# Merge gates computed inside the prompt's attention, a reordered projection, and an expert ring of sixteen slots

## The chip, the cores and the metric

The kernel runs on one core of one Trainium2 chip. The metric is the device time of one execution in microseconds (us). The time before is the median of three runs.

## The reference, cut to what matters

One layer handles a prompt of 256 tokens and eight sample tokens (T = 264 tokens together), with a model width of 1024. One input projection yields the columns of an RWKV branch (a), of a sparse-attention branch (b) and of the merge gates (g); the branches are mixed under the gates, and a mixture of 32 experts follows.

```python
def merge_and_ffn(x, y_a, y_b, p_g, w_br_a, w_br_b, w_out, norm_ffn, w_router, b_router, w_up, b_up, w_down, b_down):
    g_a, g_b = jnp.split(jax.nn.sigmoid(p_g), 2, axis=-1)
    x = x + (g_a * (y_a @ w_br_a) + g_b * (y_b @ w_br_b)) @ w_out
    return x + moe_ffn(rms_norm(x, norm_ffn), w_router, b_router, w_up, b_up, w_down, b_down)
...
        p_a, p_b, p_g = split_cols(rms_norm(xp, norm_attn[layer]) @ w_in[layer], MIX_COLS)
        y_a, wkv_p, shift_p = rwkv_branch(p_a, ...)
        y_b, cmp_p, sel_p, win_p = nsa_prompt(p_b, cw, rel_bias)
        xp = merge_and_ffn(xp, y_a, y_b, p_g, *mw)
```

`moe_ffn` sends each token to four of 32 experts; an expert is `clamped_swiglu(x @ w_up[e] + b_up[e]) @ w_down[e] + b_down[e]` with `w_up[e]` 1024x2048 (8 MB in f32) and `w_down[e]` 1024x1024 (4 MB). `nsa_prompt` attends with compressed, selected and window keys; the new window cache of the samples (`win_s`) is the old one moved by one token.

## The kernel before, in words

Everything is f32. The program is a row of stages, and each stage is a block in which every engine has its own instruction queue written out by hand; all engines meet at the end of a block. The stages in order: projection, RWKV in chunks of 64 tokens ("chunks"), compression of the cache pages, `attend_prompt`, `attend_samples`, merge, `route`, the experts, and a final norm.

**Projection** (`project`). The projected activations lie transposed in `pT[:, j, :]`, one tile j of 128 columns by 264 tokens; there are 41 tiles, 0 to 13 for branch a, 14 to 23 for branch b, 24 (GT, 24 columns) for its gates, and 25 to 40 (MT and up) for the merge gates. SP (SyncE) loads the weights two tiles at a time into `w_group`, three buffers of 1 MB. TensorE (PE) computes a tile as eight matmuls over the contraction (L460); each f32 matmul shows as two records in the trace, so a tile is 16 records. ScalarE (ACT) evicts each tile into `pT` (`evicted(a, b)`), the merge gates with a sigmoid. Between the tiles PE turns small pieces into token rows: `kv` turns (L492), `shift` turns (L498), sample rows (L507) and the token products (L520) for the chunks. Their copies out of PSUM are on VectorE (DVE); the last are fed by a long chain of elementwise work on DVE (from L399 to L412, signal `tin`), which begins when ACT has taken the square roots of `sqk`. The input of the projection is `hT`, the normed input turned, and it lives only in this stage. GpSimd (POOL) ends the stage by writing the shift states and by queueing the 4 MB copy of the window cache from DRAM to DRAM (`win_copied`).

**attend_prompt**. The 16 units are (head, half of the prompt). For the unit i, PE computes scores (L1241), DVE adds bias and takes the row maximum, ACT takes the exponentials (L1148), DVE scales, PE turns the probabilities (`turn`, L1099), ACT and DVE copy them out of PSUM to `probsT` (L1154), PE multiplies by the values (`values`, L1266 and L1268). PE's queue runs `scores(i+1)`, `turn(i)`, `values(i)`. Ahead of the units stand the compressed scores (L1221) and the turns of their probabilities `cmp_p` (L1099), whose copies to `cmp_pT` are on DVE (L1180). In the stage POOL issues 16 indirect gathers of selected cache blocks for the samples.

**attend_samples** holds `win_rows`, the window keys of eight samples (4 MB). **merge** multiplies the branch outputs, left in PSUM, with the gates on DVE, adds, and multiplies with `w_out`.

**Experts**. `B["ring"]` has twelve slots of 1 MB: eight for `w_up[e]`, four for `w_down[e]`. SP loads in the order up(1), down(0), then up(e), down(e-1); each load of a slot waits until PE has used the slot (`up_used`, `down_used`). The eight slots of up(0) are loaded in `route`. PE's queue is up(e), `turn_x(e+1)`, down(e-1) (L1964, L1945, L1982); ACT, DVE and POOL do the activation between up and down, gather the token rows and scatter the results.

## Time and profile before

| | |
|---|---|
| median of 3 runs | 1788.57 us (1782.23 to 1802.88) |
| profiled execution, own time | 1795.35 us |
| its span | 1793.5 us |
| mean granted TensorE clock, share of full | 0.901 |
| instructions | 21221 |
| busy: PE matmul, PE weight load | 1382.3 us (77%), 696.5 us (39%) |
| busy: DVE, ACT, POOL | 372.5 us (21%), 224.1 us (12%), 169.9 us (9%) |
| read from HBM, written | 484.37 MB, 16.95 MB |

The profiled execution is one of its own beside the three timed runs and is 6.8 us above their median. Stages read from the timeline: projection 0 to 213.4 us, chunks to 325.6, compression to 440.5, attend_prompt to 562.8, attend_samples to 612, merge to 693, route to 755.5, experts to 1743.2, final norm to 1793.5. In the rows, PEclk is the share of its full speed that the TensorE clock was granted, PEld is the weight load, and "idle n <- X y" names what ended n us of idle time ahead of an instruction.

### The profile page before, as it was taken

The page shows a single profiled execution, that of the slowest core. Times are in us where ns is not written, and L with a number is a line of the kernel's source. Part 1 is how long each engine was busy: PE and PEld are TensorE (multiplying, and loading weights), DVE is VectorE, ACT ScalarE, POOL GpSimd, SP SyncE. Part 2 cuts the span into 40 slices and gives each one's busy share as a digit, 9 for nine tenths or more (in the row PEclk, how much of TensorE's full clock was granted, in tenths as well). Part 3 has the DMA queues.
Part 4 walks back from the last instruction along what each step waited for, and adds up shares of the span by engine and source line. Part 5 has one row for each costly group of instructions (what it writes and reads, how often), then busy time and mean ns, then how long its engine had stood idle before and what let it go on. Part 6 is the DMA issues. An engine that isn't in the chain of part 4 may idle for free. (4 is left out here: it accounts for less than half of the span.)

```text
span 1793.5 us, 21221 instructions
## 1 busy us (share of the span) xinstructions
PE 1382.3 (77%) x8102; PEld 696.5 (39%) x8103; DVE 372.5 (21%) x792; ACT 224.1 (12%) x479; POOL 169.9 (9%) x226
## 2 busy tenths in 40 slices
PE   6978976499689595497878887887877887877870
PEld 5867876266577484332222222222222222222220
DVE  3341174311333322510101010010101010010104
ACT  2221111022122103210000000000000000000001
POOL 1000061211200000000010100000010100000010
PEclk9989988698556897599999999999999999999995
DMA  5326231531402225299999999999999999999973
GB/s 171 118 87 218 74 76 29 122 107 49 178 1 94 113 100 170 92 370 416 417 418 416 419 415 419 416 418 416 418 416 417 418 415 418 414 418 414 418 282 133
DMA packets 128400, 489.60 MB, mean 273 GB/s; under 512 B 18750, under 2 KB 50752, under 8 KB 94896
## 3 DMA queue, kind: packets, MB, share of 16 engines
q1 hardware_dynamic: 117304, 457.15, 64.8%
q0 software_dynamic: 10640, 31.11, 4.9%
q8 instruction: 41, 0.67, 0.1%
q10 hardware_dynamic: 400, 0.55, 0.1%
q14 instruction: 15, 0.12, 0.0%
HBM read 484.37 MB, written 16.95 MB: 280 GB/s over the span
## 5 line engine op out<-in xcount | busy, mean ns | idle before, releaser
L1964 PE MATMUL bank<-ex_ring,ex_xT 128*64 128x512 f32 x2048 | 495.6, 607 | 138.1 <-DMA ex_ring<-in_w_up 136.5
L1964 PEld LDWEIGHTS bank<-ex_ring,ex_xT 128*64 128x64 f32 x2048 | 126.4, 136 | 478.5 <-DMA ex_ring<-in_w_up 319.3
L1982 PE MATMUL bank<-ex_ring,ex_hT 128*64 128x512 f32 x1024 | 247.1, 604 | 47.3 <-DMA ex_ring<-in_w_down 46.6
L1921 DVE TENSOR_SCALAR ex_g<-bank 128x512 f32<-128x512 f32 x32 | 22.1, 691 | 656.8 <-PE bank L1970 656.8
L460 PE MATMUL bank<-hT,w_group 128*128 128x264 f32 (+1 forms) x656 | 153.9, 397 | 6.0 <-DMA w_group<-in_w_in 5.4
L1982 PEld LDWEIGHTS bank<-ex_ring,ex_hT 128*64 128x64 f32 x1024 | 62.4, 136 | 209.2 <-DMA ex_ring<-in_w_down 128.2
L460 PEld LDWEIGHTS bank<-hT,w_group 128*128 128x128 f32 (+1 forms) x656 | 126.3, 194 | 31.0 <-DMA w_group<-in_w_in 5.8
L1866 POOL DMA_INDIRECT scratch_choice<-ex_y,ex_di x32 | 33.3, 1040 | 675.1 <-ACT ex_y L1896 675.1
L1882 ACT ACTIVATE ex_xT<-bank 128x512 f32<-128x512 f32 x33 | 19.7, 597 | 337.7 <-PE bank L1945 337.7
L1886 ACT ACTIVATE ex_hT<-bank 128x512 f32<-128x512 f32 x32 | 19.1, 597 | 311.2 <-PE bank L1951 301.1
L1896 ACT ACTIVATE ex_y<-bank 128x512 f32<-128x512 f32 x32 | 19.1, 597 | 266.4 <-PE bank L1987 266.4
L1932 DVE COPY ex_pick_down<-ex_pick 96x64 bf16 x31 | 5.9, 191 | 223.0 <-PE bank L1987 223.0
L1858 POOL DMA_INDIRECT ex_xg<-scratch_h,ex_si x33 | 34.5, 1045 | 41.1 <-POOL ex_si L1853 24.3
L306 ACT ACTIVATE pT<-bank 128x264 f32<-128x264 f32 (+1 forms) x41 | 15.6, 389 | 150.2 <-PE bank L460 150.2
L1241 PE MATMUL bank<-pT 64*128 64x128 f32 (+1 forms) x64 | 26.0, 562 | 9.8 <-DVE cmp_pT L1180 9.8
L1266 PE MATMUL bank<-kvtok,probsT 128*128 128x64 f32 x96 | 24.7, 430 | 9.3 <-ACT probsT L1154 9.3
L1009 DVE COPY pT<-bank 128x256 f32<-128x256 f32 x32 | 13.6, 425 | 87.0 <-PE bank L1080 86.7
L1573 PE MATMUL bank<-mixed,w_out_sb 128*128 128x264 f32 x128 | 28.7, 387 | 1.5 <-DVE mixed L1547 1.5
L1080 PE MATMUL bank<-masks,x 128*128 128x128 f32 x96 | 18.7, 328 | 14.4 <-PEq L120 14.4
L1080 PE MATMUL bank<-masks,blocks 128*128 128x128 f32 x160 | 29.5, 309 | 0.0
L1565 PE MATMUL bank<-yaT,w_branches 128*128 128x264 f32 x64 | 17.5, 421 | 14.4 <-DMA w_branches<-in_w_br_b 14.4
L1945 PE MATMUL bank<-masks,ex_xg 128*128 128x128 f32 x132 | 22.1, 291 | 7.6 <-DMA ex_xg<-scratch_h,ex_si 7.6
(456 smaller groups left out, 1362.0 us busy)
## 6 DMA issues: line engine op xcount, KB each, us to landing
ex_ring<-in_w_up SPq DMA_DIRECT2D x256, 1024.0 KB, 17.2
ex_ring<-in_w_down SPq DMA_DIRECT2D x256, 512.0 KB, 18.2
w_group<-in_w_in SPq DMA_DIRECT2D x20, 1024.0 KB, 5.1
win_rows<-in_state_win_kv SPq DMA_DIRECT2D x8, 512.0 KB, 7.3
w_out_sb<-in_w_out SPq DMA_DIRECT2D x1, 4096.0 KB
choice_rows<-scratch_choice SPq DMA_DIRECT2D x2, 2048.0 KB
out_win_s<-in_state_win_kv POOLq DMA_DIRECT2D x1, 4088.0 KB, 24.2
x<-in_x_prompt SPq DMA_DIRECT2D x4, 512.0 KB
```

The source lines that it names most:

```text
L460: mm = mmul(banks[2 + i % 4][0:n, 0:T], w[:, g % 3, kc, c:c + n], hT[:, kc, :], start=(kc == 0), stop=(kc == KD - 1))
L1080: mm = mmul(banks[u % 3][:, P * t:P * t + P], raw[p % 3][:, t, c0:c0 + P], ident, start=True, stop=True)
L1241: mm = mmul(banks[i % 2][:, TP * br:TP * br + P * (tt + 1)], qg[gs, r, P * tt:P * tt + P], pT[gs, KVT + 2 + 2 * br, 0:P * (tt + 1)], start ...
L1266: mmul(b[:, HD * br:HD * br + HD], pTs[:, i % 2, c:c + P], kvtok[:, kt, 384 + 256 * br + HD * g:384 + 256 * br + HD * g + HD], start=(kt = ...
L1573: mm = mmul(banks[m % 2][:, 0:T], wo[:, c, P * m:P * m + P], mix[:, c, :], start=(c == 0), stop=(c == KD - 1))
L1858: pool.indirect_dma_start(B["xg"][:], None, halves(scratch["h"]), bass.IndirectOffsetOnAxis(ap=B["si"][:, 0:1], axis=0), bounds_check=last ...
L1866: pool.indirect_dma_start(halves(scratch["choice"]), bass.IndirectOffsetOnAxis(ap=B["di"][:, 0:1], axis=0), B["y"][:], None, bounds_check= ...
L1882: nc.scalar.activation(B["xT"][:].rearrange("p a b -> p (a b)"), banks[6][:], ACT.Copy).then_inc(S["xT_ready"], 1)
L1921: nc.vector.tensor_scalar(g[:], banks[0][:], 7.0, None, ALU.min).then_inc(S["g_ready"], 1)
L1945: mm = nc.tensor.transpose(banks[6][:, P * k:P * k + P], B["xg"][:, P * k:P * k + P], ident)
L1964: mm = mmul(banks[n // 2][lo:lo + SLOTS, :], B["xT"][:, k % 4, SLOTS * (k // 4):SLOTS * (k // 4) + SLOTS], B["ring"][:, k, 512 * n:512 * n ...
L1982: mm = mmul(banks[4][SLOTS * n:SLOTS * n + SLOTS, :], B["hT"][:, k % 4, SLOTS * (k // 4):SLOTS * (k // 4) + SLOTS], B["ring"][:, 8 + j, D ...
```

## The change

- The 16 merge-gate tiles leave the projection. `hT` is kept up to the attention. In `attend_prompt` SP loads the gate weights, 1 MB for two tiles, into the two halves of `w_cmp` (the compression's first weight), and PE computes gate tiles 0 to 2 after the compressed scores, tile 3 after the turns of `cmp_p`, and tiles 4 to 15 one in each of the units 0 to 11, between `turn(i)` and `values(i)`. ACT evicts them with tanh(x/2), and the merge makes the sigmoid of it: DVE adds 1 in the same instruction that multiplies, and the half goes into the next eviction's scale.
- In the projection ACT takes the square roots after 14 tiles instead of 18; PE turns the shift states after tile 19 and ahead of the kv turns, which come after the last tile.
- The 4 MB window copy moves from the end of the projection to the start of the chunk stage, ahead of POOL's first work there.
- `Dg` of the chunks and one buffer of the compression lie in the free gate tiles of `pT`; two of the eight samples' windows lie in `hT`, and their loads follow in the same order.
- The ring has 16 slots: eight for up, two times four for down. `route` loads down(0) as well as up(0), down(1) is issued as the experts start, and SP's order is then up(e), down(e). The expert loop on PE and SP runs in pairs. The small buffers share one array, which is also the room for the routed rows `h`, and `hit` shares `h_T`.

```diff
+            C["hT"] = sb(front, "hT", [P, KD, T])
...
-                hT = sb(st, "hT", [P, KD, T])
+                hT = C["hT"]
...
-                groups = [[12, 13], *([j, j + 1] for j in (4, 6, 0, 2, 8, 10, 18, 20, 22, 14, 16)), [GT], *([j, j + 1] for j in range(MT, NT, 2))]
...
                 group_of = {j: g for g, ts in enumerate(groups) for j in ts}
...
-                    pool.dma_start(o["win_s"][0, :, 0:511].rearrange("b t a g d -> b (t a g d)"),
-                                   a["state_win_kv"][0, :, 1:512].rearrange("b t a g d -> b (t a g d)")).then_inc(win_copied, 16)
...
-                    evicted(10, 18)
+                    evicted(10, 14)
...
+                    evicted(14, 17)
...
-                    evicted(18, 33)
+                    evicted(17, 25)
                     for i, dst in enumerate((vt, av[:, :, 0, :], br[:, :, 0, :], ktt)):
-                        evicted(33 + 2 * i, 35 + 2 * i)
...
-                    projected(14, 22)
-                    pe.wait_ge(evict, 20)
+                    projected(14, 20)
                     pe.wait_ge(kks, 4)
+                    for i in range(4):
+                        for j in range(min(4, NA_T - 4 * i)):
+                            mm = nc.tensor.transpose(banks[aux[i]][0:9, P * j:P * j + P], pT[:, 4 * i + j, TP - 1:T], ident)
+                        mm.then_inc(shp, 1)
+                    projected(20, 25)
                     for i in range(6):
                         t0, n = TILES[i // 2]
-                        if i >= 4:
+                        if i < 4:
+                            pe.wait_ge(sh_ok, i + 1)
+                        else:
                             pe.wait_ge(kv_ok, i - 3)
                         for j in range(3):
                             mm = nc.tensor.transpose(banks[aux[i % 4]][0:n, P * j:P * j + P], pT[:, KVT + 3 * (i % 2) + j, t0:t0 + n], ident)
                         mm.then_inc(kvp, 1)
-                    projected(22, 25)
-                    pe.wait_ge(kv_ok, 6)
-                    for i in range(4):
-                        for j in range(min(4, NA_T - 4 * i)):
-                            mm = nc.tensor.transpose(banks[aux[i]][0:9, P * j:P * j + P], pT[:, 4 * i + j, TP - 1:T], ident)
-                        mm.then_inc(shp, 1)
```

```diff
-                    projected(25, 29)
-                    pe.wait_ge(sh_ok, 4)
                     pe.wait_ge(smr.sem, 1)
                     for i, src in enumerate((wsm[:], kk[:, :, TP:T], cum[:, :, TP:T], q["k2"][:, :, TP:T], v[:, :, TP:T], r[:, :, TP:T])):
...
-                    pe.wait_ge(sm_ok, 6)
...
-                        projected(33 + 2 * i, 35 + 2 * i)
...
+                            else:
+                                pe.wait_ge(sm_ok, (5, 6, 3, 4)[2 * i + tt])
...
+                    pool.dma_start(o["win_s"][0, :, 0:511].rearrange("b t a g d -> b (t a g d)"),
+                                   a["state_win_kv"][0, :, 1:512].rearrange("b t a g d -> b (t a g d)")).then_inc(win_copied, 16)
                     pool.wait_ge(C["idx_ok"], 8)
                     cmp_piece(pool, 0)
...
+                w = C["w1"][:].rearrange("p a b c -> p (a b c)").rearrange("p (r k n) -> p r k n", r=2, k=KD)
...
+                NG, AHEAD = NT - MT, 4
+                gate_bank = lambda t: banks[4 + t % 2] if t < AHEAD else banks[6 + t % 2]
...
+                    for g in range(NG // 2):
+                        if g >= 2:
+                            sp.wait_ge(mtd, 2 * (g - 1))
+                        c0 = 3096 + 256 * g
+                        sp.dma_start(w[:, g % 2], a["w_in"][0][:, c0:c0 + 256].rearrange("(k p) n -> p k n", p=P)).then_inc(w_in[g % 2], 16)
...
+                    def gate(t):
+                        act.wait_ge(mtd, t + 1)
+                        nc.scalar.activation(pT[:, MT + t, :], gate_bank(t)[:, 0:T], ACT.Tanh, scale=0.5).then_inc(mte, 1)
+
+                    gate(0)
                     act.wait_ge(cx, 1)
                     nc.scalar.activation(pc[:].rearrange("p a b c d -> p (a b c d)"), pc[:].rearrange("p a b c d -> p (a b c d)"), ACT.Exp).then_inc(cxe, 1)
+                    for t in range(1, AHEAD):
+                        gate(t)
...
+                        if 1 <= i <= NG - AHEAD:
+                            gate(AHEAD + i - 1)
...
+                    def gate(t, lo, hi):
+                        if lo == 0:
+                            pe.wait_ge(w_in[t // 2 % 2], 16 * (t // 4 + 1))
+                            if t >= 2 and t != AHEAD and t != AHEAD + 1:
+                                pe.wait_ge(mte, t - 1)
+                        for kc in range(lo, hi):
+                            mm = mmul(gate_bank(t)[:, 0:T], w[:, t // 2 % 2, kc, P * (t % 2):P * (t % 2) + P], C["hT"][:, kc, :], start=(kc == 0), stop=(kc == KD - 1))
+                        if hi == KD:
+                            mm.then_inc(mtd, 1)
+
+                    for t in range(AHEAD - 1):
+                        gate(t, 0, KD)
                     pe.wait_ge(cp, 1)
                     for j in range(4):
                         if j >= 2:
...
+                    gate(AHEAD - 1, 0, KD)
...
                             pe.wait_ge(oe, i - 1)
+                        else:
+                            pe.wait_ge(mte, AHEAD - 1 + i)
...
                         turn(i)
+                        if i < NG - AHEAD:
+                            gate(AHEAD + i, 0, KD)
                         values(i)
...
+                        step(stt(ta[:, m % 2, :], pT[:, MT + m, :], 1.0, banks[2 * (m % 2)][:, 0:T], ALU.add, ALU.mult))
```

```diff
+            work = sb(moe, "ex_work", [P, 8, 512])
+            for name, shape, dt in (("ring", [P, 16, 2 * FF], F32), ("bias", [96, 3 * FF], BF16), ("pick", [96, NEXP + 1], BF16),
...
+            S["ring_in"] = [sem(f"ring_in{i}") for i in range(16)]
...
                     for k in range(8):
                         sp.dma_start(B["ring"][:, k, :], a["w_up"][0][0, P * k:P * k + P, :]).then_inc(S["ring_in"][k], 16)
+                    for k in range(8):
+                        sp.dma_start(B["ring"][:, 8 + k // 2, D * (k % 2):D * (k % 2) + D], a["w_down"][0][0, P * k:P * k + P, :]).then_inc(S["ring_in"][8 + k // 2], 16)
...
-                    def down(e, wait):
+                    def down(e, half, wait):
                         for j in range(4):
+                            slot = 8 + 4 * half + j
                             if wait:
-                                sp.wait_ge(S["down_used"], 4 * (e - 1) + j + 1)
+                                sp.wait_ge(S["down_used"], 4 * (e - 2) + j + 1)
                             for c in range(2):
                                 r0 = 256 * j + P * c
-                                sp.dma_start(B["ring"][:, 8 + j, D * c:D * c + D],
+                                sp.dma_start(B["ring"][:, slot, D * c:D * c + D],
                                              a["w_down"][0][bass.ds(e, 1), r0:r0 + P, :].rearrange("e p n -> (e p) n")
-                                             ).then_inc(ring_in[8 + j], 16)
-
+                                             ).then_inc(ring_in[slot], 16)
+
+                    down(1, 1, False)
                     up(1, True)
-                    down(0, False)
-                    with sp.Fori(2, NEXP) as e:
-                        up(e, True)
-                        down(e - 1, True)
-                    down(NEXP - 1, True)
+                    with sp.Fori(1, NEXP // 2) as pair:
+                        for half in range(2):
+                            up(2 * pair + half, True)
+                            down(2 * pair + half, half, True)
 
```

How the instructions stand in each engine's queue shows in what follows; each line is the program's line, the operation, its output and input, and its count. A matmul of the order is two records in the trace.

TensorE in the projection before, from tile 14 on. `w_group` marks projection tiles (eight matmuls a tile), L492 the kv turns, L498 the shift turns, L507 the sample rows, L520 the token products:

```order
L460 MATMUL bank<-hT,w_group 128x264 x64
L492 MATMUL bank<-masks,pT 128x128 x12
L492 MATMUL bank<-masks,pT 8x128 x6
L460 MATMUL bank<-hT,w_group 128x264 x16
L460 MATMUL bank<-hT,w_group 24x264 x8
L498 MATMUL bank<-masks,pT 9x128 x14
L460 MATMUL bank<-hT,w_group 128x264 x32
L507 MATMUL bank<-masks,sample_decay 8x128 x4
L507 MATMUL bank<-masks,w_cmp 8x128 x8
L507 MATMUL bank<-masks,rw_k 8x128 x4
L507 MATMUL bank<-masks,shifted 8x128 x8
L460 MATMUL bank<-hT,w_group 128x264 x48
```
and after, the same stretch (L459 tiles, L487 shift turns, L497 kv turns):

```order
L482 MATMUL bank<-rw_at_rt,masks 128x264 x4
L459 MATMUL bank<-hT,w_group 128x264 x48
L487 MATMUL bank<-masks,pT 9x128 x14
L459 MATMUL bank<-hT,w_group 128x264 x32
L459 MATMUL bank<-hT,w_group 24x264 x8
L497 MATMUL bank<-masks,pT 128x128 x12
L497 MATMUL bank<-masks,pT 8x128 x6
L508 MATMUL bank<-masks,sample_decay 8x128 x4
L508 MATMUL bank<-masks,w_cmp 8x128 x8
L508 MATMUL bank<-masks,rw_k 8x128 x4
L508 MATMUL bank<-masks,shifted 8x128 x8
L520 MATMUL bank<-masks,shifted 64x64 x32
```
The groups of 48, 32 and 16 gate matmuls that stood between the rows and between the products are gone, and the shift turns stand ahead of tile 20.

TensorE at the start of the prompt's attention before (L1221 compressed scores, L1099 turns, L1241 scores, L1266 and L1268 values):

```order
L1221 MATMUL bank<-KcT,pT 128x8 x16
L1099 MATMUL bank<-masks,cmp_p 8x128 x16
L1241 MATMUL bank<-pT 128x128 x2
L1241 MATMUL bank<-pT 128x256 x2
L1099 MATMUL bank<-masks,scores 128x128 x2
L1266 MATMUL bank<-kvtok,probsT 128x64 x2
L1268 MATMUL bank<-Vc,cmp_pT 128x64
L1241 MATMUL bank<-pT 128x128 x2
```
and after (L1242, L1101, L1276, L1303 and L1305 in the same roles; L1251 is a gate tile, with its weights in `w_cmp`):

```order
L1242 MATMUL bank<-KcT,pT 128x8 x16
L1251 MATMUL bank<-hT,w_cmp 128x264 x24
L1101 MATMUL bank<-masks,cmp_p 8x128 x16
L1251 MATMUL bank<-hT,w_cmp 128x264 x8
L1276 MATMUL bank<-pT 128x128 x2
L1276 MATMUL bank<-pT 128x256 x2
L1101 MATMUL bank<-masks,scores 128x128 x2
L1251 MATMUL bank<-hT,w_cmp 128x264 x8
L1303 MATMUL bank<-kvtok,probsT 128x64 x2
L1305 MATMUL bank<-Vc,cmp_pT 128x64
```
Three tiles stand ahead of the turns of `cmp_p`, one behind them, and one in every unit between its turns and its values.

ScalarE in the same stage after (L1155 is the gate's eviction by tanh, L1159 and L1167 are exponentials, L1175 is the copy to `probsT`):

```order
L1155 ACTIVATE pT<-bank 128x264
L1159 ACT_TABLE_LOAD
L1159 ACTIVATE cmp_p<-cmp_p 128x128
L1155 ACTIVATE pT<-bank 128x264 x3
L1167 ACTIVATE scores,row_sum<-scores,row_max 128x128 x2
L1175 ACTIVATE probsT<-bank 128x256
L1167 ACTIVATE scores,row_sum<-scores,row_max 128x256 x2
L1155 ACTIVATE pT<-bank 128x264
L1175 ACTIVATE probsT<-bank 128x512
```
The gate's evictions stand one behind each unit's exponentials, ahead of the copy; there is one table load in the stage, as before.

SyncE around the start of the experts before, and then after:

```order
L1646 DMA ex_ring<-in_w_up 128x2048 x8
L1649 DMA scratch_h<-h_rows 128x1024 x2
L1649 DMA scratch_h<-h_rows 8x1024
L1604 UNCONDITIONAL_BRANCH
L1818 UNCONDITIONAL_BRANCH
L1824 DMA ex_ring<-in_w_up 128x2048 x8
L1833 DMA ex_ring<-in_w_down 128x1024 x8
```
```order
L1691 DMA ex_ring<-in_w_up 128x2048 x8
L1693 DMA ex_ring<-in_w_down 128x1024 x8
L1696 DMA scratch_h<-ex_work 128x1024 x2
L1696 DMA scratch_h<-ex_work 8x1024
L1649 UNCONDITIONAL_BRANCH
L1865 UNCONDITIONAL_BRANCH
L1881 DMA ex_ring<-in_w_down 128x1024 x8
L1871 DMA ex_ring<-in_w_up 128x2048 x8
```
The eight loads of down(0) now stand in `route` ahead of the rows' store, and the first loads of the experts' block are those of a down weight instead of an up weight.

## Rows read from the trace of the kernel before

**Rows 1.** Windows: length; busy (x) of PE, PEld, DVE, ACT, POOL; PEclk; DMA share; GB/s.
```profile
110.60:213.40 102.80, 87.56 (x616) 71.31 (x616) 20.28 (x28) 12.89 (x30) 1.67 (x3) 0.92 0.40 133
...
467.50:562.80 95.30, 84.77 (x288) 67.87 (x288) 35.19 (x112) 22.48 (x80) 0.00 (x0) 0.50 0.02 9
```

**Rows 2.** Timeline of the projection: start, us, engine, line.
```profile
81.93 18.41 PE L460 MATMUL bank<-hT,w_group 128*128 128x264 f32 x82
...
99.41 0.71 DVE L399 TENSOR_SCALAR rw_at_rt<-rw_at_rt 128x1056 f32<-128x1056 f32 x1 [17.49 <-ACT rw_at_rt L334]
119.20 1.22 DVE L412 TENSOR_TENSOR rw_a<-rw_bt_kt,chunk_decay 128x1024 f32<-128x1024 f32 x1
121.08 1.44 PE L492 MATMUL bank<-masks,pT 128*8 128x128 f32 x6 [7.63 <-DVE kvtok L416]
...
151.30 3.67 DVE L423 COPY pT<-bank 8x512 f32<-8x512 f32 x6 [13.57 <-PE bank L507]
165.94 16.54 PE L460 MATMUL bank<-hT,w_group 128*128 128x264 f32 x64 [5.37 <-DMA w_group<-in_w_in]
...
182.41 2.08 PE L520 MATMUL bank<-masks,shifted 64*64 64x64 f32 x64
```

**Rows 3.** Window of 10 us inside the projection.
```profile
60.00:70.00 10.00, 10.00 (x47) 8.54 (x46) 5.85 (x13) 2.67 (x7) 0.00 (x0) 1.00 0.50 166
```

**Rows 4.** Timeline of the chunk stage.
```profile
219.31 1.13 DVE L672 TENSOR_SCALAR block_rows<-pages,cols 128x2 uint32<-128x2 int32 x8 [5.78 <-DMA cols<-in_c_cols]
255.45 3.93 POOL L650 TENSOR_TENSOR rw_bt_kt<-sample_sa,sample_vec 128x2048 f32<-128x2048 f32 x1 [14.33 <-DVE sample_sa L711]
```

**Rows 5.** The weight loads L252 from 120 to 170 us.
```profile
DMA to landing us min/median/max: 4.9/11.4/18.0
```

**Rows 6.** Timeline at the start of the prompt's attention.
```profile
440.52 6.13 PE L1221 MATMUL bank<-KcT,pT 64*128 64x8 f32 x32 [1.01 <-PEq L913]
451.40 6.29 PE L1099 MATMUL bank<-masks,cmp_p 128*8 128x128 f32 x32 [4.75 <-DVE cmp_p L1177]
466.77 0.68 DVE L1180 COPY cmp_pT<-bank 8x512 f32<-8x512 f32 x1 [7.06 <-DMA out_shift_s<-bt_tok_rb]
467.51 2.93 PE L1241 MATMUL bank<-pT 64*128 64x128 f32 x8 [9.83 <-DVE cmp_pT L1180]
```

**Rows 7.** Windows after the turns L1099 of cmp_p, while TensorE is idle.
```profile
458.00:460.00 2.00, 0.00 (x0) 0.00 (x0) 0.68 (x1) 0.00 (x0) 1.39 (x3) 1.00 1.02 418
460.00:462.00 2.00, 0.00 (x0) 0.00 (x0) 0.00 (x0) 0.00 (x0) 1.70 (x2) 0.56 1.04 418
```

**Rows 8.** Windows: one pair of units; a dense stretch of turns.
```profile
480.45:492.23 11.78, 10.62 (x38) 8.50 (x37) 4.39 (x14) 2.81 (x10) 0.00 (x0) 0.50 0.00 0
570.00:580.00 10.00, 10.00 (x89) 9.04 (x89) 4.29 (x10) 3.11 (x7) 0.00 (x0) 1.00 0.55 224
```

**Rows 9.** Waits inside the sixteen units: total, times, longest.
```profile
PE bank L1266 <- ACT probsT L1154: 9.3, 16, 0.7
```

**Rows 10.** Windows from the end of routing to the last load.
```profile
728.00:755.50 27.50, 9.17 (x42) 8.29 (x42) 19.28 (x50) 2.76 (x1) 0.00 (x0) 0.50 0.00 1
755.50:766.50 11.00, 5.69 (x16) 2.19 (x18) 0.70 (x2) 0.60 (x1) 3.25 (x6) 0.50 0.07 20
766.50:1720.00 953.50, 772.96 (x3422) 219.67 (x3418) 91.56 (x185) 72.37 (x124) 75.27 (x122) 1.00 1.02 416
1720.00:1741.20 21.20, 17.05 (x80) 5.15 (x80) 2.96 (x6) 2.22 (x4) 1.23 (x2) 1.00 0.75 278
```

**Rows 11.** Timeline of the experts' end on TensorE.
```profile
1720.36 1.94 PE L1964 MATMUL bank<-ex_ring,ex_xT 128*64 128x512 f32 x8 [0.39 <-DMA ex_ring<-in_w_up]
1723.25 1.94 PE L1982 MATMUL bank<-ex_ring,ex_hT 128*64 128x512 f32 x8
1733.89 3.65 PE L1982 MATMUL bank<-ex_ring,ex_hT 128*64 128x512 f32 x16 [0.69 <-ACT ex_hT L1886]
1741.18 1.94 PE L1982 MATMUL bank<-ex_ring,ex_hT 128*64 128x512 f32 x8 [1.18 <-DMA ex_ring<-in_w_down]
```

79 lines of the change are left out of this document (45 added, 34 removed).

## The prediction

> **What bounds the kernel now.** I read the windows by stage first, then the timelines at the places that the change touches, then the waits. In the projection TensorE is busy 87.6 of the 102.8 us from 110.6 on, at nearly its full clock [rows 1]: it is the bound there, and DMA has room. In the prompt's attention it is the bound too, 84.8 of 95.3 us for the 16 units, but at a granted clock of 0.50 [rows 1]. In the experts TensorE has slack and DMA has none: a share of 1.02 at 416 GB/s for 953 us [rows 10]. So a matmul taken out of the projection counts fully, a matmul put into the attention counts unless the clock rises, and in the experts only bytes, and the stretches in which DMA stands still, count.
>
> **Part A, the projection.** At full clock TensorE does 47 records in 10 us [rows 3], 213 ns each. A gate tile is 16 records, 3.41 us, and 16 tiles are 54.6 us. Beside them two waits of TensorE end with tile groups: 7.63 us for DVE's kv copies, which stand behind the long DVE chain, and 5.37 us for a gate weight [rows 2]. The new end, step by step:
> - Tile 14 starts near 83.3 (the group of 82 records that starts at 81.93 [rows 2] holds 6 records of the square sums). Six tiles take 20.5: 103.8. The 14 shift turns take about 1.7: 105.5. DVE's chain starts four tiles earlier, since ACT takes the roots four evictions earlier: its first row moves from 99.41 to about 85.8 and its last from 119.2, 1.2 us long, to an end at 106.8 [rows 2]. It is over before anyone waits long.
> - Tiles 20 to 24 take 17.1: 122.6. The kv turns and their six DVE copies end near 127, the sample rows with their six copies (3.67 us [rows 2]) near 131.
> - Eight token products are 4 x 2.08 = 8.3 us [rows 2]; with the copies behind the last the stage ends near 141.
>
> That is 141 in place of 213.4: **-72.5 us**. If the copies are exposed at each step the end is 147, so the term lies between -66 and -75.
>
> **Part B, the chunk stage.** The 4 MB window copy took 24.2 us to landing and slowed the loads that ran beside it: the five weight loads between 120 and 170 us took up to 18.0 us against 4.9 at best [rows 5]. Now it is issued as the chunks start. DVE's first work waits there for a small load, `cols`, already now 5.8 us [rows 4]; with 4 MB ahead it can come later by 0 to 8 us. What hides it: POOL, behind which the copy is queued, has an idle time of 14.3 us for a later value of DVE [rows 4], and TensorE, which sets this stage's end, starts on data that are in place. I take **+3**.
>
> **Part C, the prompt's attention.** The start: the compressed scores end at 446.7 [rows 6]. Tiles 0 to 2, the first at half clock and the rest at full, take 6.8 + 3.4 + 3.4 = 13.6 and cover TensorE's 4.75 us wait for `cmp_p`; the turns take 3.6 (32 records of 112 ns) to 6.3 [rows 6, 8], tile 3 another 3.4: 467.3 to 470. Today the first scores start at 467.5 although the turns are over at 457.7: DVE's copies waited 7.06 us more, while DMA ran full with the 16 gathers, and TensorE 9.83 us [rows 6]. If the copies are no longer stalled, tile 3 hides them and the scores start at 467.3; if the stall comes whole behind the later turns, near 478.6. No row tells which; I take the middle, 472.5: **+5**.
>
> The units: a pair takes 11.78 us now, with 38 records seen (36 must be the average pair's matmuls, two records each) at clock 0.50 [rows 8]. TensorE has pauses there, 16 of them for ACT's copy to `probsT`, 9.3 us in all [rows 9], and small ones; the clock stays at 0.50 for the whole stretch. With a gate tile between turn and values, ACT's and DVE's steps (2.81 and 4.39 us in a pair [rows 8]) lie under it, and TensorE has no reason to pause. Right behind the units, where turns run without pause, the clock is 1.00 and 89 records take 10 us, 112 ns each [rows 8]. At that clock a pair is 36 x 0.112 = 4.0, plus two tiles 6.8, plus about 0.6 for what is not overlapped: 11.5 in place of 11.78. Twelve units are 69 in place of 70.7; the last four, which have no tile and may keep some of the higher clock, 20 in place of 23.5. Together **-5**. So the stage is worth 0, and the 54.6 us of gate work are free there, **if the clock rises**. For that: after the turns of `cmp_p` the clock was still 1.00 for 2 us in which TensorE did nothing, and 0.56 later [rows 7], so a dense run of this sort lifts it. Bounds with the clock up: -12 to +15.
>
> Here the Trainium skill speaks for both sides. In "TensorE: Matmul & The Clock Gate", Part 1, it says that the throttled clock is the default and that activity releases it, which the rows above bear out; its section on a second failure mode warns that frequent micro-idles keep the clock from settling. [...]
>
> In attend_samples the window loads come later in SP's queue and their users later still: 0. In the merge DVE's add and multiply is one instruction as the multiply was, over the same elements: 0.
>
> **Part D, the experts.** Today DMA stands nearly still from 728 to 766.5 (1 and 20 GB/s), since every load waits for a free slot, and in the last 21 us it runs at 278 GB/s [rows 10]. From 755.5 on it moves 0.22 + 396.7 + 5.9 = 402.8 MB. After: down(0), 4.2 MB, is loaded in the idle stretch at the end of routing, at no cost (the store of `h` is queued behind it, but 4.2 MB at 416 GB/s are 10 us of 27.5); down(1) starts at once, near 757.2, and 398.5 MB are left. Up(31) is the last but one in the order, and its last slot lands at 757.2 + 394.3 MB / 416 GB/s + 1.5 = 1706.5. Behind it TensorE has 2.9 us of up (1723.25 less 1720.36), down(30) with 7.3 (2 x 3.65), about 1.3 for turning and ACT, and down(31) with 7.3 [rows 11]: 1725.3. Before, up's last slot was used at 1720.36 and the stage ended at 1743.2, 22.9 us later, with a wait of 1.18 us for the last load [rows 11]. The difference is 18; I take one off for gathers that compete with the full queue: **-17**, between -19 and -12. TensorE's work for an expert, 773 us over 31.5 experts or 24.5 us at full clock [rows 10], stays under the 30.2 us that 12.6 MB take.
>
> **Sum:** -72.5 + 3 + 5 - 5 - 17 = -86.5 against the profiled execution, 1795.35: 1708.9. That execution is 6.8 us above the median; on the median, 1788.57, it is **1702**.
>
> **Rivals.**
> 1. *The clock stays at half in the attention.* For it: it stayed at 0.50 for 95 us with TensorE busy 89% [rows 1]; against: the pauses go. A tile then costs 6.83, a pair 11.78 less its waits plus 13.7, some 23.5, so six pairs are 70 us longer, and the first four tiles 13: 1702 + 83 = 1785, no change. 6%.
> 2. *The clock swings, or the copies of `cmp_p` wait longer for DMA*, since POOL's gathers and SP's gate weights run together: a third of that, +28, 1730. 9%. In "SBUF — State Buffer" the Trainium skill holds that DVE and GpSimd share a port and one can lock out the other; DVE's stall of 7.06 us with POOL issuing gathers agrees, without telling this cause from full DMA.
> 3. *The experts' gain does not come*, because the loads that lead are given back by a lower rate: 17 less, 1719. 10%.
> 4. *Slower.* With DMA ahead by a deeper ring, TensorE's idle time for an expert comes in one piece, behind down(e-1), in place of short waits for slots. If that lets the clock fall, and the up part (4 x 3.65 = 14.6 us [rows 11]) runs at half, an expert takes 24.5 + 14.6 = 39.1 in place of 30.2: 31 x 8.9 = +276, some 1978. It decides from 86.5 / 31 = 2.8 us an expert, so from 33 us of work. Against: the clock was 1.00 from 766 to 1720 with TensorE busy 81% [rows 10]. 3%.
>
> **How the numbers follow.** My forecast has 72% for itself with its bounds, 1685 to 1722 (A +6 to -3, B -3 to +5, C -12 to +15, D -2 to +5, which do not all fall on one side). The range is 1683 to 1740; it takes in rivals 2 and 3. Repeats of the kernel spread from 1782 to 1803, so 1% is about what a measurement of it can tell. Faster by more than that: all but rivals 1 and 4, 0.91; within 1%: 0.06; slower: 0.03.
>
> **What would show it.** In the trace after: the projection ends at 141 and DVE's chain at 107; DVE's first wait in the chunks is 6 to 14 us; the first scores start 32 us (27 before) after the stage's start; the granted clock is near 1.00 in the units with tiles, at 5.75 us a unit, and no wait on `probsT`; loads of the experts' block begin within 2 us of its start, and the stage takes 970 us in place of 987.7. Wrong if the clock in the units is near 0.5, or if there is a new wait between tile and values, or if the expert stage is as long as before.

## The result and the profile after

The changed kernel takes 1738.6 us (median of 4 runs, 1734.5 to 1746.7) against 1793.7 for the kernel before, measured beside it: a ratio of 0.970, 95% interval 0.963 to 0.978, 55 us less. The forecast was 1702, within 1683 to 1740, from a base of 1788.6; it asked for 86 us less. The measured time lies inside that range, at its slow end, but the sum behind the forecast is off by 33 us, as shown below. The span of the profiled execution is 1740.4 us; before it was 1793.5.

The changed projection, from the timeline (start, duration, engine, line; in brackets the idle time before and its releaser), as [rows 2] before:

```profile
83.08 0.71 DVE L398 TENSOR_SCALAR rw_at_rt<-rw_at_rt 128x1056 f32<-128x1056 f32 x1 [1.47 <-ACT rw_at_rt L333]
105.17 1.22 DVE L411 TENSOR_TENSOR rw_a<-rw_bt_kt,chunk_decay 128x1024 f32<-128x1024 f32 x1
125.65 0.60 PE L508 MATMUL bank<-masks,sample_decay 128*8 128x128 f32 x4 [0.95 <-DVE kvtok L419]
135.12 2.06 PE L520 MATMUL bank<-masks,rw_a 64*64 64x64 f32 x64
138.13 1.15 PE L754 MATMUL bank<-rw_bt_kt,rw_at_rt 64*64 64x64 f32 x32 [0.94 <-PEq L205]
```

The stage ends at 138.1 where 141 was forecast, and the waits of 7.63 and 5.37 us are gone. The chunk stage, as [rows 4] before:

```profile
162.78 1.14 DVE L674 TENSOR_SCALAR block_rows<-pages,cols 128x2 uint32<-128x2 int32 x8 [24.56 <-DMA cols<-in_c_cols]
166.70 1.97 PE L773 MATMUL bank<-m_Y,m_level_wu 64*64 64x64 f32 x32 [21.25 <-DVE m_Y L693]
```

DVE's first work waits 24.56 us for `cols`, not 5.78, and TensorE waits 21.25 us for what DVE has queued behind it. The start of the attention, and its units, as [rows 6] and [rows 8]; a window row is length, busy time and record count of PE, PEld, DVE, ACT and POOL, the granted clock, DMA share and GB/s:

```profile
414.16 3.73 PE L1101 MATMUL bank<-masks,cmp_p 128*8 128x128 f32 x32
417.92 0.68 DVE L1201 COPY cmp_pT<-bank 8x512 f32<-8x512 f32 x1 [0.19 <-PE bank L1101]
421.57 1.57 PE L1276 MATMUL bank<-pT 64*128 64x128 f32 x8
```
```profile
434.00:446.50 12.50, 12.50 (x70) 10.68 (x69) 4.39 (x15) 3.62 (x13) 0.00 (x0) 1.00 0.27 85
500.84:522.00 21.16, 17.74 (x69) 14.30 (x68) 8.88 (x29) 4.88 (x16) 0.00 (x0) 0.58 0.00 1
```

The first scores start 26.4 us into the stage, without a stall of DVE's copies. A pair of units with its two tiles takes 12.50 us, TensorE without a pause at clock 1.00; the last four units, without tiles, are back near half clock. One tile and what follows it:

```profile
433.49 3.73 PE L1251 MATMUL bank<-hT,w_cmp 128*128 128x264 f32 x16
437.06 1.00 PE L1303 MATMUL bank<-kvtok,probsT 128*128 128x64 f32 x8
```

From start to start a tile takes 3.57 us; the 3.73 of its row overlap the next instruction.

The experts, as [rows 10] and [rows 11]:

```profile
714.70:725.00 10.30, 0.89 (x4) 0.72 (x4) 0.66 (x2) 0.00 (x0) 2.02 (x4) 0.50 0.90 335
725.00:730.00 5.00, 4.31 (x14) 1.30 (x14) 0.00 (x0) 0.60 (x1) 1.24 (x2) 0.54 0.49 193
730.00:1675.00 945.00, 766.61 (x3426) 234.47 (x3422) 91.62 (x185) 72.40 (x124) 75.53 (x122) 0.98 1.02 416
```
```profile
1674.97 1.94 PE L2012 MATMUL bank<-ex_ring,ex_work 128*64 128x512 f32 x8 [0.53 <-DMA ex_ring<-in_w_up]
1686.51 7.09 PE L2030 MATMUL bank<-ex_ring,ex_work 128*64 128x512 f32 x32 [0.75 <-ACT ex_work L1934]
```

DMA starts with the stage and, once most of down(1) has landed, runs at half its rate from 725 to 730, since the next loads wait until TensorE has used the first up slots; SP issues the next load at 729.6. Behind the last up load are 19 us, as forecast.

**Where the time went, by stage.** Both kernels were profiled twice, since the clock falls differently in each execution. The lengths, in us, are between the first loads that the stages issue (the last row says its own ends):

| stage | before, two profiles | after, two profiles | change of means | forecast |
|---|---|---|---|---|
| projection | 213.4, 212.9 | 138.1, 138.0 | -75.1 | -72.5 |
| chunks | 112.2, 112.3 | 128.8, 122.8 | +13.6 | +3 |
| compression | 114.9, 130.6 | 128.3, 127.9 | +5.4 | 0 |
| prompt's attention | 122.9, 123.0 (both with a stall) | 127.3, 125.1 (both without) | +3.3 | 0 |
| the same, both without the stall | 111.5 | 127.3, 125.1 | +14.7 | 0 |
| experts' start to the final norm's gather | 1003.3, 1003.9 | 991.5, 990.7 | -12.5 | -17 |

The line without the stall needs a word ahead of the experiments. DVE's late copies of `cmp_pT` in [rows 6] are not in every execution of the kernel. The later runs were made in four groups, each on one chip beside runs of the kernel before: experiments 1, 2, 4 and the changed kernel again; 7, 8, 9 and the kernel before again; 3, 5 and the first of 10; 6, 11 and the second of 10. A stall of DVE of 7 to 12 us beside the gathers is in all 7 profiles of two groups and in none of the 7 of the other two, whatever the kernel; one chip served a group of each kind, and the kernel before had medians of 1801 and 1807 us in the groups with the stall and of 1789 and 1787 in those without. The first profile of the kernel before has it, though both profiles of the changed kernel have not. The 111.5 us are from experiment 2, whose attention is that of the kernel before. With this line the changes add up to -75.1 + 13.6 + 5.4 + 14.7 - 12.5 = -53.9 us, near what is timed: -55 by the medians of the first comparison, and -55 again in the first group, which has no stall (1789.4 against one execution of the changed kernel, 1734.1).

How the 55 us divide is less sure than the sum. The first profiles of both kernels alone, the one before with the stall, give -75.3 + 16.6 + 13.4 + 4.4 - 11.8 = -52.7. Two things hold whichever profiles are taken. The chunk stage is longer. And so is the attention, like compared with like: 125.1 and 127.3 against 111.5 without the stall, and with it 135.1 (experiment 6) against 122.9, 123.0 and 123.8 (experiment 7), so 12 to 15 us.

### The profile page after: what moved, and what is told of

The parts are those of the page before. It is cut to its first block and busy times, and to the rows that moved or that the text cites. A ratio compares the mean times of both kernels' runs of the same rounds, so it can differ in the third digit from the quotient of the medians.

```text
span 1740.4 us, 21135 instructions
## 1 busy us (share of the span) xinstructions
PE 1350.9 (78%) x8102; PEld 693.3 (40%) x8103; DVE 367.7 (21%) x792; ACT 223.4 (13%) x478; POOL 170.5 (10%) x226
## 5 line engine op out<-in xcount | busy, mean ns | idle before, releaser
L2012 PE MATMUL bank<-ex_ring,ex_work 128*64 128x512 f32 x2048 | 507.1, 623 | 178.6 <-DMA ex_ring<-in_w_up 176.8
L2012 PEld LDWEIGHTS bank<-ex_ring,ex_work 128*64 128x64 f32 x2048 | 133.2, 140 | 524.5 <-DMA ex_ring<-in_w_up 308.7
L2030 PE MATMUL bank<-ex_ring,ex_work 128*64 128x512 f32 x1024 | 226.8, 595 | 0.8 <-ACT ex_work L1934 0.8
L2030 PEld LDWEIGHTS bank<-ex_ring,ex_work 128*64 128x64 f32 x1024 | 70.7, 137 | 134.1 <-issue 133.1
L1914 POOL DMA_INDIRECT scratch_choice<-ex_work,ex_di x32 | 33.4, 1043 | 665.5 <-ACT ex_work L1944 665.5
L459 PE MATMUL bank<-hT,w_group 128*128 128x264 f32 (+1 forms) x400 | 91.9, 392 | 0.6 <-DVE hT L365 0.6
L459 PEld LDWEIGHTS bank<-hT,w_group 128*128 128x128 f32 (+1 forms) x400 | 75.5, 190 | 15.8 <-issue 0.7
L1934 ACT ACTIVATE ex_work<-bank 128x512 f32<-128x512 f32 x32 | 19.1, 597 | 359.7 <-PE bank L1999 359.7
L1930 ACT ACTIVATE ex_work<-bank 128x512 f32<-128x512 f32 x33 | 19.7, 598 | 344.8 <-PE bank L1993 344.8
L1251 PE MATMUL bank<-hT,w_cmp 128*128 128x264 f32 x256 | 63.3, 404 | 0.7 <-DMA w_cmp<-in_w_in 0.7
L1251 PEld LDWEIGHTS bank<-hT,w_cmp 128*128 128x128 f32 x256 | 50.1, 200 | 9.7 <-DMA w_cmp<-in_w_in 0.9
L1944 ACT ACTIVATE ex_work<-bank 128x512 f32<-128x512 f32 x32 | 19.1, 597 | 202.2 <-PE bank L2035 202.2
L1906 POOL DMA_INDIRECT ex_work<-scratch_h,ex_si x33 | 34.6, 1049 | 40.3 <-POOL ex_si L1901 24.3
L773 PE MATMUL bank<-m_Y,m_level_wu 64*64 64x64 f32 x320 | 13.7, 246 | 27.8 <-DVE m_Y L693 21.2
L1011 DVE COPY pT<-bank 128x256 f32<-128x256 f32 x32 | 13.6, 425 | 99.7 <-PE bank L1082 99.6
L1046 PE MATMUL bank<-pT,w_cmp 64*128 64x265 f32 x128 | 29.9, 553 | 0.4 <-DVE pT L1014 0.4
L1606 PE MATMUL bank<-yaT,w_branches 128*128 128x264 f32 x64 | 17.5, 421 | 14.4 <-DMA w_branches<-in_w_br_b 14.4
## 6 DMA issues: line engine op xcount, KB each, us to landing
out_win_s<-in_state_win_kv POOLq DMA_DIRECT2D x1, 4088.0 KB, 23.5
```

The source lines that it names most:

```text
L459: mm = mmul(banks[2 + i % 4][0:n, 0:T], w[:, g % 3, kc, c:c + n], hT[:, kc, :], start=(kc == 0), stop=(kc == KD - 1))
L1046: mmul(banks[4 + 2 * kv + g][:, 0:T + 1], w1[r // 16][gs, kv, r % 16, :], fl[gs, u % 4, :], start=(r == 0), stop=(r == 31)).then_inc(hid, 1)
L1251: mm = mmul(gate_bank(t)[:, 0:T], w[:, t // 2 % 2, kc, P * (t % 2):P * (t % 2) + P], C["hT"][:, kc, :], start=(kc == 0), stop=(kc == KD - 1))
L1906: pool.indirect_dma_start(B["xg"][:], None, halves(scratch["h"]), bass.IndirectOffsetOnAxis(ap=B["si"][:, 0:1], axis=0), bounds_check=last ...
L1914: pool.indirect_dma_start(halves(scratch["choice"]), bass.IndirectOffsetOnAxis(ap=B["di"][:, 0:1], axis=0), B["y"][:], None, bounds_check= ...
L1930: nc.scalar.activation(B["xT"][:].rearrange("p a b -> p (a b)"), banks[6][:], ACT.Copy).then_inc(S["xT_ready"], 1)
```

## The experiments

Ratios are to the kernel before, run beside each on the same chip; the changed kernel's is 0.970. 0.1% is 1.8 us. The changed kernel's ratio was measured apart from the others and has an interval of 0.0075 to either side, 13 us, so a difference of 7 us between two ratios is not resolved; the readings rest on the stage lengths and waits, which are from one profile of each. The expectations count the chunk stage to TensorE's last matmul in it, and the compression from there, about 14 us ahead of the first load: their 109 to 116 and 141 us are the 122.8 to 128.8 and 128 of the table.

**1. The window copy back at the end of the projection** (e1_copy_back).

```diff
 # chunks, POOL
-                    pool.dma_start(o["win_s"]..., a["state_win_kv"]...).then_inc(win_copied, 16)
 # projection, POOL, behind the shift states
+                    pool.dma_start(o["win_s"]..., a["state_win_kv"]...).then_inc(win_copied, 16)
```

> The changed kernel with one part undone: the 4 MB window copy is queued behind the shift states at the end of the projection again. Theory (the chunks' small load `cols` is stuck behind the copy, 24.6 us in the changed kernel against 5.8): the copy lands before the chunks start, DVE's first wait in the chunk stage falls to 5 to 8 us, that stage shortens by 17 to 19 us, and the whole to about 1720. Rival (the wait has another cause, such as the projection's late output stores, which now come right ahead of the chunk stage): the wait stays near 24 us and the time near 1738.

Measured: 0.9591 (0.9527 to 0.9656), 1716.6 us: 1.1% or 20 us less than the change. The chunk stage takes 103.0 us:

```profile
145.31 1.14 DVE L674 TENSOR_SCALAR block_rows<-pages,cols 128x2 uint32<-128x2 int32 x8 [4.40 <-DMA cols<-in_c_cols]
```

The wait is 4.40 us. The projection's stage grows by 2.7 us (138.1 to 140.8), which is all that the copy costs there. The theory holds; the rival is out. The later profiles agree: the chunk stage takes 98.9 to 111.0 us in the five versions with the copy back, and 122.7 to 130.0 in the six profiles of the changed kernel and its versions with the copy at its start. By their means the copy costs 22 us there. That is more than the 13.6 of the table, since the stage without it is some 8 us shorter than the 112.2 of the kernel before; the cause of that is not shown.

**2. The copy's move alone, on the kernel before** (e4_copy_alone).

> The kernel before with one part of the change alone: the window copy moved from the end of the projection to the start of the chunk stage. Theory: DVE's wait for `cols` grows from 5.8 to about 24 us and TensorE's wait for a gate weight in the projection (5.4 us) goes, so 10 to 14 us slower than before, about 1806. Rival (the copy is hidden there, and the long wait in the changed kernel comes from the shorter projection): same as before, within 3 us.

Measured: 1.0058 (1.0021 to 1.0096), 10 us slower. In its profile the wait for `cols` is 24.7 us, the projection is 6.6 us shorter and the chunk stage 11.3 us longer (123.5). The stages give 4.7 us of the 10; the interval reaches from 4 to 17. (Its span, 1787.8, is below that of the first profile of the kernel before all the same: its attention has no stall and takes 111.5 us.) The first scores start at 461.40, 16.7 us into the attention:

```profile
461.40 1.57 PE L1241 MATMUL bank<-pT 64*128 64x128 f32 x8 [0.77 <-DVE cmp_pT L1180]
```

So the move is a loss by itself, in either surroundings.

**3. The copy in the chunk stage, but behind the small loads** (e8_copy_behind_small_loads).

```diff
+                    pool.wait_ge(pg_in, 48)
                     pool.dma_start(o["win_s"]..., a["state_win_kv"]...).then_inc(win_copied, 16)
```

> The changed kernel with one wait added: in the chunk stage POOL issues the window copy only when `pages` and `cols` have landed. Theory (a few hundred bytes stuck behind 4 MB are the whole harm): DVE's first wait falls from 24.6 to about 6 us, the chunk stage from 109 to 116 us to about 95, though the copy still runs in it; the whole 13 to 18 us faster than the changed kernel, close to the version with the copy back in the projection. Rival (the later loads of the stage, samples' vectors and states, then wait in place of `cols`): the stage stays above 105 us.

Measured: 0.9662 (0.9628 to 0.9696), 7 us less than the change, not 13 to 18. The stage takes 116.5 us, or 102 as the expectation counts, between the theory's 95 and the rival's 105. The waits (who waited on what, total, times, longest):

```profile
POOL rw_bt_kt L650 <- DMA sample_val<-scratch_rwkv_in: 18.4, 1, 18.4
DVE sample_sa L714 <- POOL rw_bt_kt L650: 9.1, 1, 9.1
DVE block_rows L675 <- DMA cols<-in_c_cols: 5.7, 1, 5.7
```

`cols` is on time (5.7), but the samples' vectors now stand behind the copy, POOL waits for them, and DVE for POOL. That is the rival's mechanism: it is not one load alone, the stage's other early loads have no room for the 4 MB either.

**4. rel_bias ahead of the late weights** (e2_rel_first). In both kernels TensorE waits 11.8 to 14.4 us in the compression for a tiny load behind 2 MB, and then runs at half clock for a while. In the changed kernel:

```profile
289.29 1.87 PE L1057 MATMUL bank<-yb_tok,rel_bias 32*8 32x512 f32 x2 [11.94 <-DMA rel_bias<-in_rel_bias]
289.30:322.90 33.60, 33.60 (x106) 17.73 (x106) 4.77 (x16) 2.90 (x12) 3.76 (x4) 0.50 0.27 86
```

```diff
-                    cmp_weights(sp, w1[1], 1, w_late)
                     sp.dma_start(rel[:], a["rel_bias"]).then_inc(hin, 16)
+                    cmp_weights(sp, w1[1], 1, w_late)
```

> The changed kernel with one thing added: in the compression stage the tiny load of rel_bias is issued ahead of the four loads of late weights (2 MB), not behind them. Theory (TensorE's 11.9 us of idle time for rel_bias in that stage is what throws its clock to half, and the clock then stays at half for 34 us): the idle time falls under 3 us, the granted clock stays near 1.00, and the stage loses 12 us of waiting and 13 us of half speed: some 25 us, 1714. Rival (the half clock does not hang on that idle time): 12 us or less, 1727, with a stretch near 0.50 still in the stage.

Measured: 0.9605 (0.954 to 0.967), 17 us less than the change. The profile shows the compression at 98.9 us, 29 less, with full clock nearly throughout, but the mean gain is between the 12 of the rival and the 25 of the theory. One profile was not enough to decide that: the version of experiment 9 has no such wait either, and its clock is at half all the same.

**5. The wait kept, but filled with work** (e7_filled_wait).

```diff
                             if i == 0:
+                                for _ in range(26):
+                                    mmul(banks[3][:, 0:T], ident, pT[:, QT, :], start=True, stop=True)
                                 pe.wait_ge(hin, 32)
```

> The changed kernel with 26 extra matmuls, whose result is overwritten unread, ahead of TensorE's wait for rel_bias in the compression stage: the load comes as late as before, but TensorE works instead of standing idle. Theory (the idle time costs twice, once as a wait and again as half clock behind it): rel_bias is used as late as before, the granted clock is 1.00 behind it, and the compression stage takes 125 to 130 us in place of 141; the whole 10 to 15 us faster than the changed kernel. Rival (only the wait itself counts, and the clock's fall has another cause): 141 us and no gain.

Measured: 0.9707 (0.9674 to 0.9741): no gain, and a compression of 126.4 us. A miss. Windows of the compression:

```profile
277.20:289.80 12.60, 11.88 (x55) 9.80 (x53) 0.00 (x0) 0.00 (x0) 0.00 (x0) 1.00 0.96 202
289.80:336.10 46.30, 46.30 (x281) 27.57 (x281) 9.80 (x36) 10.88 (x40) 7.50 (x8) 1.00 0.40 127
341.00:372.00 31.00, 31.00 (x109) 18.66 (x105) 3.23 (x14) 3.38 (x14) 1.63 (x2) 0.50 0.11 34
```

The clock did stay at 1.00 through the wait and for 46 us behind it, where the changed kernel has 33.6 us at 0.50. But then it fell with TensorE busy all the time, and 31 us at half took the gain back. What stands between the last two windows is one group:

```profile
336.11 3.73 PE L1072 MATMUL bank<-rel_bias,yb_tok 32*128 32x8 f32 x32
```

These are 16 products with eight output columns. In the changed kernel too the clock is 0.50 for 6 us right behind them (355 to 361). In all 14 profiles of the study in which they stand in one piece a stretch of half clock follows, of about 3 to 33 us, with TensorE busy.

**6. Those 16 products spread, two in each of eight units of the compression's loop** (e11_products_spread on the changed kernel).

```diff
+                        if 39 <= u <= 46:
+                            block_bias(u - 39)      # two of the 16 products; the last one signals
```

> The changed kernel, in the compression stage the 16 products with eight output columns (block bias, 3.7 to 4.1 us in one piece) are spread over eight units, two in each. Theory (the clock falls to half behind that piece, for 6 to 30 us): from the first rise on the clock stays near 1.00 to the end of the stage, the stage takes 4 to 15 us less than 141, and the whole is 0.2 to 0.8% faster than the changed kernel. Rival (the clock falls at some place in any case): the same time, a half stretch elsewhere.

Measured: 0.9623 (0.9578 to 0.9669), 0.8% or 14 us less than the change. In its profile:

```profile
287.60:323.00 35.40, 35.34 (x112) 19.25 (x114) 5.15 (x18) 3.28 (x13) 3.76 (x4) 0.50 0.31 99
323.00:390.00 67.00, 65.75 (x421) 42.81 (x419) 12.12 (x50) 16.26 (x56) 5.63 (x6) 1.00 0.17 52
```

Behind the wait the half stretch is there as ever, and from its end on the clock is 1.00 to the end of the stage. That is what the theory of a second trigger asked for. The profile itself gained only 3 us (125.1), as the changed kernel's happened to have a short second stretch; the 14 us are the mean over executions, and the intervals overlap, so the gain by itself is not shown; experiment 11 has a closer comparison.

**7. The ring of sixteen slots alone, on the kernel before** (e5_ring_alone).

> The kernel before with the part of the experts alone: sixteen slots, down(0) loaded while routing, down(1) first, pairs. Theory (the ring's share of the measured gain is 12 to 13 us, since DMA still stands idle 4 us before the first slot of up comes free): 12 to 13 us faster than before. Rival (the prediction's 17 us are there, and the missing four come from the attention's side): 16 to 18 us faster.

Measured: 0.9934 (0.9888 to 0.998), 12 us less (4 to 20); from the experts' start to the final norm's gather 990.7 us, against 1003.3 and 1003.9. The part's gain is 12 to 13 us wherever it is applied.

**8. The unit tiles left out** (e6_no_unit_gates).

```diff
-                        if i < NG - AHEAD:
-                            gate(AHEAD + i, 0, KD)
```

With the tiles go their six weight loads and their evictions; this kernel sets those gates to zero and leaves their part out of the output.

> The changed kernel with gate tiles 4 to 15 left out (neither their weights are loaded nor are they computed; those gates are zero in the output). Theory (the tile between turns and values lifts the clock, so that the work of a unit takes half the time and pays for the tile): the units fall back to a granted clock of 0.50 and about 11.8 us a pair, and the whole is only 2 to 6 us faster than the changed kernel although 45 us of matmuls are gone. Rival (the clock would be high without the tiles, from the first four gates on): pairs of some 7 us, 30 us faster.

Measured: 0.966 (0.9596 to 0.9725), 7 us less than the change, although 12 x 3.57 = 43 us of matmuls are gone. A pair of units without tiles:

```profile
457.80:469.60 11.80, 10.64 (x38) 8.52 (x37) 4.39 (x14) 2.80 (x10) 0.00 (x0) 0.50 0.00 1
```

11.8 us at 0.50, against 12.50 at 1.00 with the tiles. The four gates ahead of the units don't keep the clock up; the tile in each unit does, and it pays for itself but for 0.35 us a unit. This profile and those of 7 and 9 are of a group with the stall; here it is 12 us ahead of DVE's first copy of `cmp_pT`, so the attention as a whole (130.4 us) compares with the 135.2 of experiment 9, not with the changed kernel's 127.3: 4.8 us for the twelve tiles.

**9. Both loads put right** (e3_copy_back_rel_first: experiments 1 and 4).

> The changed kernel with both edits: the window copy back at the end of the projection, and rel_bias loaded ahead of the late weights. If the two waits are separate, their gains add: 18 and 25 us, about 1695. If the second gain is only a shift of phase of the clock, it is 12 us or less here: 1708.

Measured: 0.9495 (0.9429 to 0.956), 2.1% or 37 us less than the change: the gains of 20 and 17 add. Its profile has the stall, 12.2 us ahead of `cmp_pT`, and an attention of 135.2 us. Its compression takes 122.2 us, though `rel_bias` is on time: TensorE, busy throughout, stays at half clock for the first 45 us of the stage. The first and the last of seven windows of 6 us:

```profile
244.80:250.80 6.00, 6.00 (x24) 4.47 (x24) 3.40 (x15) 2.00 (x6) 3.80 (x4) 0.50 0.72 186
280.80:286.80 6.00, 6.00 (x22) 3.71 (x20) 1.09 (x4) 0.48 (x2) 1.87 (x2) 0.50 0.40 105
```

So the wait is not the only thing ahead of a long half stretch. With the load early the compression takes 97.7 to 122.2 us in five profiles, with it late and unfilled 112.7 to 131.5 in ten.

**10. The version of experiment 9 with the gathers behind the copies of `cmp_pT`** (e9_gathers_after_turns, and e9_again).

```diff
+                    pool.wait_ge(cpe, 4)
                     for s in range(NB):
                         for c in range(2):
                             pool.indirect_dma_start(sel[:, s, c]...)
```

> The version with the copy back and rel_bias first, and with POOL's 16 gathers of the attention issued only when DVE has copied cmp_pT. Theory (the stall of DVE and ACT of 7 to 12 us that some executions show there comes with the full DMA traffic of the gathers): no stall at those copies, the attention takes 122 to 127 us, and the whole is up to 5 us faster on the mean than without this edit. Rival (the gathers have no part in it, or they delay the gate weights by as much): same time, or a new wait of TensorE for w_cmp of several us.

> The version with the copy back, rel_bias first and the gathers behind the turns once more, on the same chip as the two above, for the comparison: 0.951 of the kernel before. By the theory of two triggers its compression stage still shows a half stretch behind the 16 products in this profile.

Measured: 0.9506 (0.9459 to 0.9552) and 0.9474 (0.943 to 0.9518), the same as without the edit. The first is of a group without the stall and tells nothing of it (attention 126.6 us). The second is of a group with it, and takes 137.2: the stall isn't gone, it moved with the gathers. The edit shows no gain, and that half of the theory which promised a gain fell. By the second profile the compression has its half stretch behind the 16 products (0.58 over 305 to 345 us), as expected there.

**11. The version of experiment 10 with the products spread as well** (e10_best_spread).

> The version with the copy back, rel_bias first and the gathers behind the turns, and with the 16 products spread as well. Theory (both triggers gone): the compression stage at full clock from its start or from its first rise on, 108 to 113 us, where the version without the spread takes 113 to 135; 5 to 10 us faster on the mean. Rival: no difference.

Measured: 0.9419 (0.937 to 0.9469), 1695.4 us, 0.55% or 10 us less than the same without the spread, run beside it. The ratios' intervals overlap, but the means of the six times of each are 12 us apart (1697.2 and 1709.5), and five of the six with it are below five of the six without. The compression takes 97.7 us (112.4 without the spread), and from its first rise on its clock does not fall:

```profile
250.00:325.00 75.00, 75.00 (x465) 47.30 (x465) 14.52 (x55) 15.71 (x60) 9.37 (x10) 1.00 0.50 136
325.00:340.00 15.00, 13.75 (x91) 8.92 (x91) 3.27 (x13) 4.81 (x13) 0.00 (x0) 1.00 0.00 1
```

The stall of DVE and ACT is in this profile too, beside the gathers, at their new place:

```profile
374.50:388.00 13.50, 5.37 (x29) 4.39 (x29) 1.93 (x7) 1.45 (x5) 7.29 (x8) 0.85 1.03 416
```
```profile
379.93 0.28 DVE L1232 TENSOR_SCALAR yb_tok<-bank,gates 128x64 f32<-128x64 f32 x1 [10.15 <-remote]
386.94 0.60 ACT L1184 ACTIVATE probsT<-bank 128x512 f32<-128x512 f32 x1 [11.65 <-remote]
```

The profile names no releaser for them but "remote"; TensorE had finished what DVE's waits for at 374.5. This is the best version of the study.

**12. Both kernels once more** (c_before_again, c_after_again).

> The kernel before once more, for a second profile: whether its compression stage again runs at full clock from 5 us after the wait for rel_bias on, and whether DVE's copy of cmp_pT again starts 9 us after the turns that it waits for.

> The changed kernel once more, for a second profile. If the 34 us of half clock in the compression stage follow from the program, they stand in this profile too, at the same place and of the same length; if they are a matter of one execution, the stretch is shorter or absent and the span some 13 us shorter.

Measured: 1812.8 and 1734.1 us, one execution each. The kernel before now has a compression of 130.6 us, 15.7 more than in its first profile, with half clock for 35 us behind the wait instead of 5; the changed kernel shows 127.9 where it showed 128.3. So the length of these stretches isn't fixed by the program, and the +5 of the compression in the table above can't be laid to the change. The kernel before is of a group with the stall here (11.1 us in two waits), the changed kernel of one without.

## Why the prediction was wrong

- **Part A** was right in mechanism and size: -75 against -72.5. The 3 us more are in its end: the token products start at 129.5, not 131, as the samples' copies are over at 130, and they and their copies take 8.6 us, not 10.
- **Part B is the step that failed.** It said that with 4 MB ahead the small load "can come later by 0 to 8 us", and that POOL's idle time hides it. The load came 19 us later, that is with the whole copy, which takes 23.3 to 24.6 us to landing in the profiles; 24.2 stood in the prediction itself. And the cover was looked for on POOL, where the copy is queued, instead of behind the engine that waits: DVE did none of the work queued behind its first until `cols` had landed, and TensorE needs its masked products from that work (21.25 us). Experiments 1, 2 and 3 show it from three sides. The stage is 13.6 us longer where 3 were given; the copy alone costs some 22 us in it (experiment 1), and 11.3 in the kernel before. Experiment 3 adds that the load of `cols` is not the only one that the copy holds up.
- **Part C is the second step that failed.** That the tiles lift the clock was right, and experiment 8 shows the units at rival 1's clock. (Rival 1's pair, 11.78 less 1.2 of waits plus 13.7, is 24.3 us, not 23.5.) But the sum set the new start against 467.5, "today the first scores start at" that time, 27 us in, and let tile 3 hide in a wait of 9.83 us that the kernel has only in executions with the stall. Without it the old start is 16.7 us long (experiment 2); the new one is 26.4: the four tiles cost 9.7 us and not 5. The pair was mis-sized by 1.0 us, 12.50 against 11.5: a tile takes 3.57, not 3.41 us, and the other 5.4 us hold 38 records, 141 ns each, where the sum took 36 of 112 ns and 0.6 us. (The 3.41 came from 47 records in a window of 10 us, which counts those that reach over its edges.) Twelve units are 4.3 us longer than before, not 1.7 shorter, and the rest of the units, with the last four at 0.58 of the clock, is about 1 us longer, not 3.5 shorter. Together +14.7 where 0 was given.
- **Part D** was -12.5, not -17. The prediction counted the stage to TensorE's last matmul, 987.7 us; so counted it is 978 to 979 after against 988 before, 9 less, and the other 3 us came behind that matmul, which the sum did not treat. The term that was mis-sized is the landing of the last up load: 951 us after the start by the sum, 960 in the trace. Some 5 us are rate: the ring starts at once, but up(1) can't be loaded before TensorE has used a slot of up(0), and TensorE waits for the first gather until 724. The same 11 us of `x` gather were in the trace before; the sum let DMA run on through it. Some 8 are order: by then DMA had moved 3.45 + 0.97 + 393.1 = 397.5 MB, not 394.3, and in the 20 us behind it it moved only 1.5 MB, so down(31), 4.2 MB, which the sum placed behind up(31), had come in for the most part. The 1.7 and 1.5 us that the sum allowed for start and landing, for which it names no row, take 3 of these 13 back. What lies behind up's last load was as forecast. TensorE's clock in the experts was 0.93 to 1.00 in stretches of 50 us where it had been 1.00 before, but DMA stayed at 416 GB/s, so the slower rival's price did not come.
- **The rest.** B is short by 10.6, C by 14.7, D by 4.5 and the compression by 5.4, less 2.6 that A gained more: 32.6 us, the difference between the forecast -86.5 and the -53.9 of the table, from which these numbers are taken. The compression's 5.4 can't be laid to the change. The range took one profile's wait and clock as the kernel's; the stage ahead varies by 15 us from profile to profile and the stall is worth 9 to 12, which alone should have widened it. That the measured time is still inside is luck in part: the range reached to 1740 for rivals 2 and 3, and in the changed kernel's profiles the clock held in the units from the second pair on, the copies of `cmp_pT` did not wait for DMA, and the rate in the experts did not fall.

## What to carry to other kernels

A large copy with no reader can hold up small loads on another queue than its own, here for its whole length: put it where no engine waits for a load soon after, as at the end of the projection here, and price it at its whole length where one does. Work that fills the pauses of an engine at half clock may be nearly free, as here 43 us of matmuls for 4 to 7 us. And a wait without a clear releaser in one profile is no cover to plan with: look at a second one first.

## What the runs showed of the hardware

- Sixteen products of eight columns, 3.7 us in one piece with TensorE busy throughout, are followed by a granted clock of 0.50 for 6 us (changed kernel), 31 us (filled wait) and about 33 us (within 305 to 345 us in the second profile of experiment 10) of otherwise dense work, and for about 3 us or more in all 14 profiles that have them so. Two at a time among the compression's units they are not, in both profiles made. What sets the length was not found.
- The granted clock can stay at 0.50 for 45 us with TensorE busy for 44.8 of them (experiment 9, from 244.5 us), and the same program shows 4.5 or 35 us of it behind the same wait (the two profiles of the kernel before).
- During the 16 gathers (8.4 MB, DMA at 418 GB/s in [rows 7]) DVE, and ACT in five of the profiles, stood still for 7 to 12 us with their inputs ready, in every profile of two groups of runs, in none of two others, and in one of the two profiles of the first comparison. It moved with the gathers. POOL issues them alike with the stall and without, and DMA is as full (412 to 418 GB/s in experiment 2). A cause that holds DVE alone would not cover ACT's stall. What decides that a group has it, and what the engines wait for, is not settled.
